# The last expert's rows stay in SBUF and join their tokens by a 0/1 product; the other rows are fetched and summed earlier

## What is computed

```
x = layer_norm(DEEPNORM_ALPHA * x + mix, ...)
# the mixture: top-1 group, then top-2 experts in it; weights = gate * softmax(top two)
h = jax.nn.silu(xb @ w_gate[e]) * (xb @ w_up[e]);  out = h @ w_down[e]
y = segment_sum(out * row_w[:, None], row_tok)        # two weighted rows for each token
x = layer_norm(DEEPNORM_ALPHA * x + y, ...)
```

## Time and profile before

| | us |
|---|---|
| median of 3 runs | 2459.82 (2459.29 to 2468.2) |
| the profiled execution, its own time | 2462.13 |
| its span, first to last instruction | 2460.4 |
| layer 0: experts' last matmuls end, first projection of layer 1 starts | 1133.47, 1186.94 |
| layer 1: experts' last matmuls end, last gain-and-bias work of POOL ends | 2398.77, 2456.01 |

### The profile page before, as it was taken

How to read it: one execution, slowest core, us unless ns; L and a number is a source line. 1 busy time by engine, 2 the same in 40 slices (tenths; PEclk the granted TensorE clock), 3 DMA queues, 4 the chain that set the end, 5 groups by cost and what they waited for, 6 DMA issues and landing times. The chain is left out here.

```text
span 2460.4 us, 33859 instructions
## 1 busy us (share of the span) xinstructions
PE 2277.2 (93%) x12788; PEld 1873.8 (76%) x12788; DVE 1797.3 (73%) x2520; ACT 1363.2 (55%) x1662; POOL 248.0 (10%) x238
## 2 busy tenths in 40 slices
PE   8999998989999999994799999989989999999990
PEld 6767886878888888883678778867778888888870
DVE  4665556568999999996555555556579999999986
ACT  3454435026777777773344444443047777777753
POOL 0000000001111111111400000000011111111105
PEclk9999999989999999996899999999999999999995
DMA  4010004229999999997311111105069999999975
GB/s 130 24 30 27 27 15 143 86 99 368 391 378 383 382 385 384 386 356 251 138 46 37 37 37 38 37 35 183 26 230 405 392 400 392 385 381 373 376 283 209
DMA packets 155146, 534.31 MB, mean 217 GB/s; under 512 B 39232, under 2 KB 79192, under 8 KB 105832
## 3 DMA queue, kind: packets, MB, share of 16 engines
q1 hardware_dynamic: 136208, 498.45, 53.9%
q0 software_dynamic: 18432, 33.60, 3.6%
q10 hardware_dynamic: 344, 0.08, 0.0%
HBM read 515.21 MB, written 50.39 MB: 230 GB/s over the span
## 5 line engine op out<-in xcount | busy, mean ns | idle before, releaser
L352 DVE TENSOR_TENSOR arena<-arena,arena 128x2048 fp32r<-128x2048 f32 (+1 forms) x458 | 955.2, 2116 | 76.9 <-ACT arena L1848 56.6
L1848 ACT CAST arena<-arena 128x2048 fp32r<-128x2048 f32 x384 | 716.1, 1917 | 134.9 <-PE psum L1625 120.1
L1625 PE MATMUL psum<-arena,arena 128*128 128x512 f32 x3072 | 734.2, 395 | 0.0
L1625 PEld LDWEIGHTS psum<-arena,arena 128*128 128x128 f32 x3072 | 569.6, 189 | 114.6 <-issue 0.4
L643 PE MATMUL psum<-arena,arena 128*128 128x512 f32 x2016 | 506.0, 401 | 8.3 <-DVE arena L352 7.6
L643 PEld LDWEIGHTS psum<-arena,arena 128*128 128x128 f32 x2016 | 369.7, 189 | 102.0 <-issue 16.2
L1636 PE MATMUL psum<-arena,arena 128*128 128x512 f32 x1536 | 365.1, 394 | 2.8 <-DVE arena L352 2.8
L1636 PEld LDWEIGHTS psum<-arena,arena 128*128 128x128 f32 x1536 | 291.6, 190 | 66.5 <-DVE arena L352 4.3
L352 DVE TENSOR_TENSOR arena<-psum,arena 128x512 fp32r<-128x512 f32 (+1 forms) x186 | 161.2, 874 | 106.3 <-ACT arena L768 55.2
L785 ACT ACTIVATE arena<-arena,arena 128x640 f32<-128x640 f32 (+4 forms) x192 | 120.0, 626 | 202.8 <-DVE arena L883 152.3
L343 PE MATMUL psum<-ident,arena 128*128 128x128 f32 x1024 | 151.0, 289 | 64.3 <-POOL arena L1017 26.7
(11 more groups left out here) (166 smaller groups left out, 1548.4 us busy)
## 6 DMA issues: line engine op xcount, KB each, us to landing
arena<-in_moe_w_gate SPq DMA_DIRECT2D x128, 1024.0 KB, 8.5
arena<-in_moe_w_up SPq DMA_DIRECT2D x128, 1024.0 KB, 7.7
arena<-in_moe_w_down SPq DMA_DIRECT2D x128, 1024.0 KB, 6.9
arena<-expert_rows SPq DMA_DIRECT2D x32, 512.0 KB, 5.3
x_rows<-arena SPq DMA_DIRECT2D x24, 512.0 KB, 2.7
arena<-x_rows SPq DMA_DIRECT2D x24, 512.0 KB, 7.2
arena<-in_c_w_in SPq DMA_DIRECT2D x24, 512.0 KB, 4.2
arena<-in_x SPq DMA_DIRECT2D x16, 512.0 KB, 7.3
```

Source lines behind the costliest of these rows:

```text
L352: return eng.tensor_tensor(tile, src, high.bitcast(F32), ALU.subtract)
L1625: mm = pe.matmul(bank(o), cs[:, c * P:(c + 1) * P], ws[:, c * FF:(c + 1) * FF], start=(k == 0 and c == 0), stop=(k == 2 and c == CH - 1))
L1848: act.copy(w_hi[w][:, cols], self.raw[w][:, cols]).then_inc(hi_ready[w], 1)
```

## The change

The last expert's result is no longer sent to HBM. ACT and DVE weigh it, straight from PSUM, into a high and a low part in SBUF (`tail_hi`, `tail_lo`), and PE adds each row to its token by a matmul with a 0/1 matrix (`picks`, made by DVE under expert 30: a slot's token compared with a row of numbers). So the other 31 experts' rows can be fetched under the last expert: SP asks for tiles 0 to 6 as soon as expert 30's rows have landed, and DVE forms each tile's partial sum (second row, then x1: `make`) in SBUF instead of PSUM, the first two under the last expert, the others three tiles ahead of their use. What the last expert's rows would read in HBM is cleared by a scatter of zeros under expert 1 (`clear_last`), and its slots' weights come by an indirect DMA from `pair_weights`, which SP writes at expert 6. The lists of further blocks are made only if there are any. All blocks end without drains. In layer 0 the last four tiles of x1 are fetched behind the rows of tile 7 (`last_rows`), since their buffers are the last expert's weights; in layer 1 two tiles are now finished by DVE alone (3 and 7) and six go through POOL.

```
-            return ctx2.enter_context(nc.Block())
+            return ctx2.enter_context(nc.Block(no_gpsimd_drain=True))
...
-        first_raw = [place(16 + 4 * i, CH * P) for i in range(3)]
+        first_raw = [place(kb, CH * P) for kb in (16, 20, 128)]
```

SP in the experts' block:

```
+                        if e == 6:
+                            sp.wait_ge(before.weights_ready, 1)
+                            with nc.allow_non_contiguous_dma(reason="2048 weights, once a layer"):
+                                sp.dma_start(w_dram.rearrange("(t p k) o -> p k (t o)", p=P, k=2), w_pair[:]
+                                             ).then_inc(w_sent, 16)
...
+                    sp.wait_ge(lo_ready[UP], 1 + 2 * EXPERTS)
+                    combine.rows_ahead(sp, 0)
+                    sp.wait_ge(y_out[0], 8 * EXPERTS)
+                    sp.wait_ge(y_out[1], 8 * EXPERTS)
+                    sp.wait_ge(xt_ready, 1 + EXPERTS)
+                    combine.fetch_rows(sp, 0)
+                    sp.wait_ge(up_done, 1 + EXPERTS - 1)
+                    combine.fetch_rows(sp, 1)
+                    sp.wait_ge(up_done, 1 + EXPERTS)
+                    combine.fetch_rows(sp, 2)
+                    sp.wait_ge(gate_done, 1 + EXPERTS)
+                    combine.fetch_rows(sp, 3)
+                    sp.wait_ge(lo_ready[DOWN], 1 + 2 * EXPERTS)
+                    combine.rows_ahead(sp, 1)
+                    for t in range(4, TILES - 1):
+                        combine.fetch_rows(sp, t)
+                    count = extra_count(sp)
+                    sp.wait_ge(down_done, ALL_DOWN)
...
-                    sp.wait_ge(down_done, 1 + EXPERTS)
-                    sp.wait_ge(before.extras_ready, 1)
-                    count = extra_blocks(sp, more)
-                    sp.wait_ge(x_w, 1 + count)
-                    settle(sp)
-                    sp.wait_ge(rows_sent, 1)
-                    combine.first_rows(sp)
...
+                    extra_blocks(sp, count, first, more, after)
+                    sp.wait_ge(tail_lo, 2)
+                    combine.last_rows(sp)
```

POOL there:

```
+                    def clear_last():
+                        pool.memset(res[1], 0.0).then_inc(cleared, 1)
+                        pool.memset(w_slot, 0.0).then_inc(cleared, 1)
+                        pool.wait_ge(cleared, 2)
+                        scatter(res[1], slot_rows[:, LAST, 1:2], y_out[1])
+                        pool.wait_ge(y_out[1], 16)
+                        pool.sem_inc(res_free, 1)
```

ACT at the last expert:

```
+                        combine.scale_first(act, 0)
+                        combine.scale_first(act, 1)
+                        act.wait_ge(x_rows_in, 16)
+                        for s in range(2):
+                            act.wait_ge(down_done, ALL_DOWN - 1 + s)
+                            act.mul(tail[0][:, s * BANK:(s + 1) * BANK], bank(B_Y + s), w_slot).then_inc(tail_hi, 1)
+                        combine.scale_first(act, 2)
...
+                    extra_blocks(act, count, first, more, after)
+                    act.activation(stats[:, 0, 19:20], ident[:, 0:1], ACT.Sqrt)
```

DVE at experts 30 and 31:

```
                             before.plan_extras(dve)
+                            pick_tokens()
                         else:
-                            before.mark_extras(dve)
...
+                            count.append(extra_count(dve))
+                            combine.make(dve, 0)
+                            combine.make(dve, 1)
...
+                        for s in range(2):
+                            cols = slice(s * BANK, (s + 1) * BANK)
+                            dve.wait_ge(tail_hi, s + 1)
+                            dve.scalar_tensor_tensor(out=tail[1][:, cols], in0=bank(B_Y + s), scalar=w_slot,
+                                                     in1=tail[0][:, cols].bitcast(F32), op0=ALU.mult,
+                                                     op1=ALU.subtract).then_inc(tail_lo, 1)
...
+                    def pick_tokens():
+                        chain.link(dve.tensor_copy(last_token, slot_rows[:, LAST, 0:1]))
+                        chain.link(dve.tensor_scalar(token_in, tile_from[:], last_token, None, ALU.add))
+                        for t in range(TILES):
+                            dve.tensor_scalar(picks[:, t * P:(t + 1) * P], iota_cols[:], token_in[:, t:t + 1], None,
+                                              ALU.is_equal)
```

The sum and the norm, class `Combine`:

```
+            def last_rows(self, sp):
+                self.fetch_rows(sp, TILES - 1)
+                for t in range(self.ahead, TILES):
+                    self.fetch_x1(sp, t, x1_late)
...
+            def x1_here(self, eng, t):
                 if t < self.ahead:
                     eng.wait_ge(x1_in[t // 4], 64 * (self.layer + 1 if t < 4 else 1))
+                else:
+                    eng.wait_ge(x1_late, 16 * (TILES - self.ahead))
...
+            def make(self, dve, t):
+                self.rows_here(dve, t)
+                self.was_scaled(dve, t)
+                self.weigh_second(dve, t).then_inc(made_half, 1)
+                self.x1_here(dve, t)
+                dve.wait_ge(made_half, MADE * self.layer + t + 1)
+                self.add_x1(dve, t).then_inc(made, 1)
...
-                whole = (TILES - 1,) if last else ()
+                whole = (3, TILES - 1) if last else ()
...
+                def sum_up(pe, t):
+                    if t >= pairs_of_banks:
+                        pe.wait_ge(added, t - pairs_of_banks + 1)
+                    pick = self.picks[:, t * P:(t + 1) * P]
+                    for s in range(2):
+                        cols = slice(s * BANK, (s + 1) * BANK)
+                        into = sum_banks(t)[:, cols]
+                        pe.matmul(into, pick, self.tail_hi[:, cols], start=True, stop=False)
+                        mm = pe.matmul(into, pick, self.tail_lo[:, cols], start=False, stop=True)
+                    mm.then_inc(summed, 1)
...
-                    scale_first(act, 0)
+                    self.scale_first(act, 3)
+                    self.scale_first(act, 4)
                     for t in range(TILES):
-                        if t + 1 < TILES:
-                            scale_first(act, t + 1)
                         if t >= 1:
                             act_norm(act, t - 1)
+                        if 1 <= t < TILES - 4:
+                            self.scale_first(act, t + 4)
+                        if not last and t in (1, 2):
+                            split_w(t - 1)
```

DVE there:

```
+                    self.make(dve, 2)
                     for t in range(TILES):
                         add(dve, t)
+                        if t + 3 < TILES:
+                            self.make(dve, t + 3)
                         if t >= 1:
                             finish(dve, chain, t - 1)
                         moments(dve, chain, t)
+                        if not last and t in (1, 2):
+                            split_w(t - 1)
                         if t >= 3 and not last:
                             keep_tile(t - 3)
+                        if not last and t == 5:
+                            split_w(2)
```

More of the change, by code:

```diff
@@ L1671, in _, with first @@
                                      ).then_inc(ln_in, 16)
+                    sp.wait_ge(lo_ready[UP], 1 + 2 * EXPERTS)
[16 more added lines that the diff above has]
+                    sp.wait_ge(down_done, ALL_DOWN)
+                    def first():
+                        sp.wait_ge(before.extras_ready, 1)
+                        for t in range(TILES - 1):
+                            combine.rows_here(sp, t)
+                        combine.early_done(sp)
                     def more(j):
@@ L1747, in more, with after @@
                         settle(pool)
-                        scatter(0, row, x_out)
+                        scatter(rows[0], row, x_out)
                         pool.wait_ge(x_out, 16 * (j + 1))
                         settle(pool)
-                    pool.wait_ge(before.extras_ready, 1)
-                    extra_blocks(pool, more)
-                    pool.sem_inc(rows_sent, 1)
+                    def after():
+                        pool.sem_inc(cleared, 1)
+                    pool.wait_ge(tail_lo, 2)
+                    extra_blocks(pool, count, first, more, after)
                 @block.tensor
@@ L1896, in more, with first, after @@
                         act.copy(h_hi, bank(B_HT)).then_inc(x_hth, 1)
[L1898 to L1900 removed]
+                    count = extra_count(act)
+                    def first():
+                        act.wait_ge(before.extras_ready, 1)
+                        combine.early_done(act)
+                    def after():
+                        act.wait_ge(w_sent, 16 + 32 * (TILES - 1))
+                        for t in range(EARLY):
+                            combine.scale(act, combine.firsts, 0, t).then_inc(tail_hi, 1)
+                    extra_blocks(act, count, first, more, after)
+                    act.activation(stats[:, 0, 19:20], ident[:, 0:1], ACT.Sqrt)
```

(6 more changed lines are left out.)

255 lines of the change are left out of this document (155 added, 100 removed).

## The result

The changed kernel is slower: 2502.53 us (2501.15 to 2503.21) against 2461.61 us, ratio 1.0162, 95% interval 1.0148 to 1.0175. The prediction had 2477 with a range up to 2486. Its profiled execution took 2502.7 us with a span of 2501.0, so the two profiled spans differ by 40.6 us, which six marks split. The first five rows end at a scatter of POOL or at a first or last matmul; "last matmul" is where the last expert's down product ends.

The account below looks back on a forecast made before the run. PE works without a gap in the experts, so the cost lies in two hand-overs of 53.5 and 57.2 us. Shifts 8.6 + 4.0 + 5.6 - 0.6 = +17.6 on the median 2459.8 give 2477.4 us; range 2460 to 2486.

Parts of the forecast that it names:

- The write of 2048 single weights at expert 6 ... so 0, at most 4 a layer: Experts: 1024 pieces took 0.67 us to issue, 3.14 at most, so the write costs 0, at most 4 us a layer.
- SP and the queues have slack: Experts, expert 6: reason given for pricing the write of 2048 single weights at 0, at most 4 us a layer.
- Rival 3: Experts: the write of single weights stalls PE, weights late by up to 4 us a layer; 2483 to 2489, chance 0.14.
- 7 us are won at each meeting: Both hand-overs: engines meet at 1138 instead of 1144.9 in layer 0, 2402.4 instead of 2409.9 in layer 1.
- Most of this is POOL's drain: Both hand-overs: ACT's 10.88 us idle until 1144.96 is mostly POOL's drain, 5.29 us in each layer.
- Layer 0 from x1 on, 40.3 + 4: Layer 0's hand-over: 40.3 us from x1's late addition to tile 3's split, plus some 4 of DVE and POOL contention.
- the wait for x1: Layer 0's hand-over: x1 lands at 1155.2, DVE waits nearly 7 us at tile 4's second addition, undoing the meeting's gain.
- Contention, +4 and +9.3: Hand-overs: DVE additions reading SBUF twice and POOL exclude each other; some +4 us in layer 0, +9.3 in layer 1.
- rival 1: Hand-overs: DVE is not held up by POOL, so +4.3 us in all, 2464.1; chance 0.26.
- Layer 1 otherwise 3.7 earlier: Layer 1's hand-over: without contention POOL's last work ends at 2452.3, 3.7 us earlier; net +5.6 with contention.
- The drains of the attention, -0.6: Attention's end: drains of 1.16 us mostly overlap the last work, so dropping them gives -0.3 us a layer, -0.6 in all.
- Picks 2.4 us, the clear at nothing: Last expert and expert 1: picks and two small steps take 2.4 us; clearing costs 0, as POOL idles there.

Follow-up runs that it names:

- the SBUF run: Kernel before, with ACT scaling first rows in place and both additions of a tile reading SBUF twice; 2499.1 us, ratio 1.0147 to the kernel before.
- the PSUM run: Changed kernel, with layer 1's partial sums of tiles 3 to 7 made in two pairs of PSUM banks; 2490.5 us, ratio 1.0119 to the kernel before.
- written late: Changed kernel, with the single weights' write moved behind the last request for an expert's weights, their gather behind expert 30's scatter; 2492.5 us, 1.0126 to before.

## Why the prediction was wrong

- **"The write of 2048 single weights at expert 6 ... so 0, at most 4 a layer"**: the step that failed most. It measured 7.9 and 8.2. I took the price from the time to issue (0.67, at most 3.14), and that was right (0.65); but the pieces are paid for in the queues, which were full: "SP and the queues have slack" stood against a share of 0.99 in the earlier trace rows. Rival 3 named the mechanism, with half the price. These are 16 of the 23 us that were missing.
- **"7 us are won at each meeting"**: failed. 0.9 us lost in layer 0 and 1.3 won in layer 1. "Most of this is POOL's drain" was misread: it is 5.29 of ACT's 10.88 us, and leaving it out alone moved layer 0's meeting by 4.3. In layer 0 the new last one is SP. Its six issues themselves took 3.8 us, but they began only at 1147.4, since the projection's weights and tile 4's rows had held SP for 9.9 us in full queues. In layer 1 it is PE, 6 us late for a reason that stays open. For layer 0 the prediction let x1 take the 7 us back anyway, so only 2.9 us of the miss lie there: x1's late tiles were asked for at 1148.3, and their addition began 24.7 behind the last matmul instead of the forecast's 21.7 (1155.2 - 1133.5). In layer 1 the forecast's hand-over is 61.6 + 5.6 = 67.2; measured 71.4, with the meeting 6.2 later than I had it.
- **Layer 0 from x1 on, 40.3 + 4**: 44.3 measured, in part by luck. With the sums in PSUM in both layers the same way takes 41.5 (1162.35 to 1203.86), so the path was 1.2 longer than forecast and contention 2.8 instead of 4. That the wait for x1 would be 7 us was wrong (1.95), because DVE came late itself.
- **Contention, +4 and +9.3**: the mechanism was right, against rival 1, and the sizes near: PSUM takes 2.4 out of layer 0's whole hand-over and 8.2 out of layer 1's. The reason was thin (one direction in one row); the SBUF run shows both. In layer 1 the three tiles take 8.4 us each and in the PSUM run 5.6, so exclusion costs 2.8 a tile where 3.1 was forecast; yet by the SBUF run, which cost 36 us where 8 to 16 were expected, the way the two engines hold each other up wasn't understood.
- **Layer 1 otherwise 3.7 earlier**: with exclusion gone it is 63.2, 1.6 longer than before. The meeting takes it, which in that run stands 9.3 behind the last matmul and not 3.6.
- **The drains of the attention, -0.6**: can't be told. The first expert is sent 1.7 us earlier, but this mark lies anywhere from 580.6 to 590.0 in the traces, and with nothing but the drains gone it came at 589.5.
- **Picks 2.4 us, the clear at nothing**: the ten instructions took 2.1 us (from 1121.51), and the scatter of zeros left no mark. Right.

Sum by the table: forecast 17.6, measured 40.6. 16.1 of the 23.0 between them are the pieces, 2.9 and 4.2 lie in the hand-overs (15.5 against 12.6, 9.8 against 5.6). Outside of these it is -0.8 where -0.6 was forecast: -1.7 at the start, +2.6 in layer 1's attention and router, where no instruction was changed, and -1.7 along the experts; such amounts also lie between two executions of one kernel (PSUM, layer 1: 2489.4 to 2499.1).

## What to carry over

Count the pieces of a transfer, not its bytes or the time to issue it, and price them where they run: 2048 pieces of 4 B cost 8 us a time beside full queues, 128 pieces of 64 B under half a microsecond. An addition whose operands both move to SBUF is a new dependence on GpSimd, even if the instruction count stays the same. And a late engine at a meeting is seldom alone: before a drain is taken for a gain, look at what every other engine, above all the one that issues transfers, still has to do, and at whether the data for the next step has landed. A hand-over read in one trace is worth no more than its marks: note where the meeting stands before a gain is put down to an edit.

## What the runs showed of the hardware

- 8 KB in pieces of 4 B held the queues at 0 to 223 GB/s for about 12 us (changed kernel, 666 to 678 us); in pieces of 64 B they moved 400 GB/s (665 to 680 us).
- A transfer of 512 KB was mostly issued in 0.43 us, but in 3.48 where it followed the projection's weights into full queues (changed kernel, 1140.17), and in 6.54 right behind the small pieces (written late, 1102.32).
- POOL's steps of 2.35 and DVE's of 1.2 become 3.20 and 3.24 to 3.31 in strict turns where both read SBUF twice (before with SBUF additions, layer 1): 8.38 us a tile, some 3.6 more than the 4.7 of POOL alone, without a single added instruction.
- POOL's drain at a block's end took 5.29 us. Without it the engines met 4.3 us earlier in layer 0, and the kernel's time was the same within 0.2% (0.9984 to 1.0006).
